# Gated linear attention heads: when a weight chunk is rounded, when each exponential signals, and the order of the gated output's chunks

## The reference, cut to what matters

```
q, k, v, r = split(h @ w_in)                      # 4 heads, dk = 128, dv = 256
log_a = log_sigmoid((h @ w_a1) @ w_a2 + b_a) / 16
b = cumsum(log_a)
scores[i,j] = sum_d q[i,d] k[j,d] exp(b[i,d] - b[j,d])    (j <= i)
o = scores @ v + (q * exp(b)) @ S ;  S_new = exp(b_last) * S + (k * exp(b_last - b))^T v
out = (rmsnorm(o, out_norm) * silu(r)) @ w_out ;  x = x + out
```

## Time and profile before

| | us |
|---|---|
| median of the timed runs | 2563.43 |
| lowest and highest of the three | 2563.18, 2563.78 |
| the profiled execution's own time | 2564.44 |
| its span, first to last instruction | 2562.7 |
| TensorE busy (share of the span) | 2506.0 (98%) |
| VectorE, ScalarE, GpSimd busy | 1640.9, 1054.4, 803.7 |

### The profile page before, as it was taken

One profiled execution on the slowest core, in us unless ns is written; L12 is line 12 of the kernel. 1 busy time (PEld: TensorE's weight loads), 2 busy tenths in 40 slices (PEclk: granted clock), 3 DMA queues, 4 the chain that ended last, 5 costly groups with the idle time before them and its releaser, 6 DMA issues.

```text
span 2562.7 us, 44016 instructions
## 1 busy us (share of the span) xinstructions
PE 2506.0 (98%) x18342; PEld 2426.2 (95%) x18342; DVE 1640.9 (64%) x2666; ACT 1054.4 (41%) x1737; POOL 803.7 (31%) x532
## 2 busy tenths in 40 slices
PE   8999999999999999999999999999999999999999
PEld 6899999998999999999998998999999999999999
DVE  6735353588676756774725786665697676748754
ACT  6433342473233333332537666445553233333322
POOL 5221222253444444003522214333434444441002
PEclk9999999999999999999999999999999999999999
DMA  3111111032332326352213444122223332336522
GB/s 113 40 34 40 34 40 50 24 111 82 109 108 95 124 94 217 111 168 76 72 36 111 138 177 164 60 85 76 74 69 98 112 109 97 122 113 224 168 80 82
DMA packets 229682, 252.25 MB, mean 98 GB/s; under 512 B 16849, under 2 KB 178271, under 8 KB 228591
## 3 DMA queue, kind: packets, MB, share of 16 engines
q1 hardware_dynamic: 227087, 247.36, 29.4%
q10 hardware_dynamic: 2400, 2.10, 0.3%
HBM read 173.54 MB, written 75.89 MB: 97 GB/s over the span
## 4 chain that ended last, share of the span: by engine, by line
PE 79%; DVE 14%; issue 3%; ACT 2%; DMA 1%; SPq 0%; POOL 0%; DVEq 0%; ACTq 0%; POOLq 0%
PE ps L905 13%; PE ps L907 13%; PE ps L906 13%; PE ps L348 8%; PE ps L350 8%; PE ps L349 8%; PE ps L2836 3%; PE ps L2821 1%; PE ps L1713 1%; PE ps L1714 1%; PE ps L1715 1%; DVE xT L1432 1%; PE ps L1726 1%; DVE hflat L493 1%; PE ps L1808 1%
## 5 line engine op out<-in xcount | busy, mean ns | idle before, releaser
L1580 POOL TENSOR_TENSOR wlo<-wraw,whi 128x1024 fp32r<-128x1024 f32 x78 | 192.4, 2466 | 440.1 <-DVE s_raw L1267 440.1
L905 PE MATMUL ps<-hh,whi 128*128 128x264 f32 x928 | 264.8, 285 | 6.1 <-DVE wlo L1308 3.8
L313 POOL TENSOR_TENSOR wlo<-wraw,whi 128x2048 fp32r<-128x2048 f32 (+1 forms) x21 | 94.3, 4491 | 553.4 <-ACT whi L306 524.0
L906 PE MATMUL ps<-hl,whi 128*128 128x264 f32 x928 | 263.9, 284 | 0.0
L907 PE MATMUL ps<-hh,wlo 128*128 128x264 f32 x928 | 263.9, 284 | 0.0
L348 PE MATMUL ps<-hh,whi 128*128 128x352 f32 x648 | 218.8, 338 | 0.6 <-ACT cqr L3171 0.3
L592 DVE TENSOR_TENSOR xT<-xT,ps 128x352 f32<-128x352 f32 x288 | 147.2, 518 | 98.2 <-PE ps L350 97.7
L350 PE MATMUL ps<-hh,wlo 128*128 128x352 f32 x648 | 208.1, 321 | 0.0
L349 PE MATMUL ps<-hl,whi 128*128 128x352 f32 x648 | 207.9, 321 | 0.0
L905 PEld LDWEIGHTS ps<-hh,whi 128*128 128x128 f32 x928 | 174.7, 188 | 7.9 <-DVE wlo L1308 5.2
L1580 POOL TENSOR_TENSOR s_lo<-s_raw,s_hi 128x512 fp32r<-128x512 f32 x80 | 157.8, 1973 | 60.0 <-ACT s_hi L1101 60.0
(11 more groups left out here) (471 smaller groups left out, 8636.2 us busy)
## 6 DMA issues: line engine op xcount, KB each, us to landing
wraw<-w_ffn_in SPq DMA_DIRECT2D x88, 512.0 KB, 3.8
s_a<-hf SPq DMA_DIRECT2D x44, 528.0 KB, 3.2
wraw<-w_ffn_out SPq DMA_DIRECT2D x44, 512.0 KB, 3.8
s_t<-h SPq DMA_DIRECT2D x16, 1056.0 KB, 4.5
hflat<-s_t SPq DMA_DIRECT2D x16, 1056.0 KB, 6.0
h<-s_a SPq DMA_DIRECT2D x12, 1056.0 KB, 5.8
wraw<-w_gla_in SPq DMA_DIRECT2D x24, 512.0 KB, 4.5
s_x<-xT SPq DMA_DIRECT2D x6, 1408.0 KB, 5.5
```

What stands on the lines that cost most here:

```text
L313: pool.tensor_tensor(lo[:, 0:cols], raw[:, 0:cols], hi[:, 0:cols].bitcast(F32), ALU.subtract).then_inc(S("w_lo"), 1)
L905: nc.tensor.matmul(out, w_[0], x_[0], start=first, stop=False, skip_group_check=True)
L906: nc.tensor.matmul(out, w_[0], x_[1], start=False, stop=False, skip_group_check=True)
L1580: return pool.tensor_tensor(lo[:, cols], raw[:, cols], hi[:, cols].bitcast(F32), ALU.subtract)
```

## The change

On ScalarE each of the two exponentials of a level signals `lvl_exp`, so that the semaphore counts 14 a head; the split of `gc(h, 2)` stands between the exponentials of level 2 and `v_copy(3)`; and `ga_hi(1)` stands ahead of `silu(1, 2)`. On VectorE `lvl_qk` waits for the first exponential ahead of the queries' product and for the second ahead of the keys'; and the gated output is worked on in the order product 0, product 1, low 0, low 1, product 2, low 2. No instruction that computes is added or taken out.

```diff
@@ act_gla_decays
-            act.activation(v[:, :, hl_:2 * hl_], v[:, :, hl_:2 * hl_], ACT.Exp, scale=1.0 / TAU)
+            act.activation(v[:, :, hl_:2 * hl_], v[:, :, hl_:2 * hl_], ACT.Exp, scale=1.0 / TAU)\
+               .then_inc(S("lvl_exp"), 1)
             act.activation(v[:, :, 0:hl_], v[:, :, 0:hl_], ACT.Exp, scale=-1.0 / TAU)\
                .then_inc(S("lvl_exp"), 1)
@@ act_gla_head
                 act_gla_decays(act, h, n_)
-                v_copy(n_ + 1)
                 if n_ == 2:
                     act_split(act, gc(h, 2), WC)
+                v_copy(n_ + 1)
...
             ga_hi(0)
+            ga_hi(1)
             silu(1, 2)
-            ga_hi(1)
             ga_hi(2)
@@ lvl_qk
-                dve.wait_ge(S("lvl_exp"), h * 7 + n_ + 1)
+                dve.wait_ge(S("lvl_exp"), h * 14 + 2 * n_ + 1)
...
                 dve.tensor_tensor(scaled[:, :, hl_:2 * hl_], blocks(gq[:, 0, :], hl_, n)[:, :, hl_:2 * hl_],
                                   e[:, :, hl_:2 * hl_], ALU.mult)
+                dve.wait_ge(S("lvl_exp"), h * 14 + 2 * n_ + 2)
@@ dve_gla_head
-            for j in range(NCH):
+            def gated(j):
...
+            def gated_low(j):
...
+            gated(0)
+            gated(1)
+            gated_low(0)
+            gated_low(1)
+            gated(2)
+            gated_low(2)
```

## The result

The changed kernel takes 2549.29 us (median of 5 runs, 2548.74 to 2549.97) against 2563.58 for the kernel before (5 runs, 2563.18 to 2564.14): a ratio of 0.9943, 95% interval 0.9933 to 0.9954, 14.3 us less. I had forecast 2551.8, and 2549.5 to 2557.0 for the range: the direction and the places were right, the gain was 2.7 us larger than the sum of 11.6, and the median lies 0.2 us outside the range. Two single executions among the experiments, 4077 us in e6 and 6300 us in e11, are far outside all the others and count in no ratio. Its profiled execution took 2549.7 us with a span of 2547.9, where the one before had 2564.44 and 2562.7.

The account below looks back on a forecast made before the run. TensorE, busy 98% of the span, was taken as the bound, so only its waits could be gained: 8.3 + 0.6 + 2.7 = 11.6 us off the 2563.43 us median gives 2551.8 us; range 2549.5 to 2557.0.

Parts of the forecast that it names:

- The wait at level 3: Head 1: TensorE's 1.47 us wait, traced to ScalarE's split delaying the exponentials; moving the split removes it, 0.9 us to spare.
- Part 2: Levels: each exponential signals alone, queries' product starts some 0.54 us earlier; VectorE's extra wait priced at 0, at most 0.12.
- Heads 1 to 3: Waits at levels 3 and 4 hold 8.6 us; less 0.1 us left in each head, gain 8.3 us.
- Head 0: Levels with a scan behind every iteration: VectorE is the bound from level 3 on; gain 0.6 us, ends -0.5 and 3.3.
- Part 3: Gated output reordered: xT waits in the output projection go, 2.4 us plus 0.3 on top of four waits, 2.7 us.
- Given back: Rival: gains are waited out later, behind the heads; half left, 2557.6 us, or up to no change, 2563; chance 0.11.
- slower: Rival: GpSimd's eight subtractions each take their longest against VectorE's level products; 5.3 us slower, 2568.7 us; chance 0.03.
- not what it says: Rival: level 3's differences are late, not the split, so its exponentials start no earlier; held excluded, no chance given.
- The turns eat part 1: Rival, levels 3 and 4: VectorE's two-SBUF-input product also passes a subtraction, each level 0.65 us later; 2556.8 us, chance 0.20.

Follow-up runs that it names:

- e6: Kernel before with only VectorE's new order of the gated output, ScalarE's order as before: 2563.47 us.
- e11: Changed kernel with GpSimd's eight subtractions held back until level 5's products are made: 2547.38 us.
- e1: Kernel before with only the split of the r chunk moved ahead of v_copy(3): 2557.29 us.
- e2: Kernel before with only the signals changed, each exponential signalling alone: 2559.48 us.
- e0: Kernel before, unchanged, run again for a second profile: 2563.53 us.
- e13: Changed kernel, unchanged, run again for a second profile: 2549.71 us.
- e7: Changed kernel with GpSimd's low part of the r chunk in 4 subtractions of 512 columns instead of 8 of 256: 2550.48 us.
- e12: Changed kernel with five of head 0's six scans put behind the product with exp(b), eight subtractions kept: 2545.76 us.
- e9: Changed kernel with four of head 0's six scans, those behind iterations 2 to 5, moved behind the product with exp(b): 2548.57 us.
- e8: Changed kernel with the low part of the r chunk in 16 subtractions of 128 columns: 2547.79 us.

## Why the prediction was right, and where it was short

- **The wait at level 3, and its source**: right. The split fills the idle time in front of `v_copy(3)`, which starts on its tile; the exponentials start behind the copy; e1 without e2 leaves 0.18 us of the 1.47.
- **Part 2, the extra wait at no cost**: right. Between L2067 and L2072 no gap opened (0.78 + 208.66 = 209.44 against a start at 209.36). e2 alone gains 4.1 us.
- **Heads 1 to 3**: 8.3 forecast, 8.77 measured (3.02, 2.74, 3.01), 0.5 short. I had kept 0.1 us of wait at level 4 of each; nothing is left. Head 2's lower figure comes from a level 4 wait of only 0.52 us in the first profile of before; in the second (e0) it was 1.1, like the others, and the stage 0.3 longer.
- **Head 0**: 0.6 forecast, 1.24 and 1.15 measured, 0.6 short. "VectorE is the bound from level 3 on" was right only together with the turns: levels 4 to 6 of the changed kernel start 4.26 and 4.25 us apart, VectorE's pace, but in e11 levels 3 to 5 keep TensorE's 4.11 with every scan in place. This was the term with the widest ends, -0.5 to 3.3. Its upper end alone gives 2549.1 us, which is below my range (2549.5) and far below the 2550 of the forecast's own.
- **Part 3**: 2.7 us forecast, 3.4 measured between the first profiles (0.62, 0.63, 0.62, 1.49) and 3.6 alone. **This is the step that failed.** I wrote "0.3 for what comes on top of four waits", having worked out 0.25 us for each wait in the levels and used it for the six waits of heads 1 to 3 just before. Four waits make 1.0: the term is 3.4, as measured. The mechanism was right, and this term of the sum too small by 0.7 us.
- **The remainder**: 13.56 us of the 14.3 between the medians are gained up to the first L905 in the first two profiles, 0.19 of it ahead of head 0's levels, where the second profile of before stands 0.16 us the other way, so that is spread too. The other 0.7 is in no stage that the change touches. The second pair of medians (e13) does not have it: its gain is 13.4.
- **The sum**: 0.7 for part 3, 0.6 for head 0, 0.5 for heads 1 to 3, 0.2 and 0.7 of the remainder make the 2.7 us by which 11.6 fell short. With 1.0 in place of 0.3 the forecast would have been 2551.1. Whether the median came to lie just outside or just inside the range was luck, as the two sets of runs show; that part 3 came out at 2.7 was not.
- **Given back, slower, not what it says**: none. No new wait of TensorE has come in the heads. Behind them one has grown, at L348 for the low part of the latent queries, from 0.7 us to 0.4 and 1.6. It is the execution's and not the change's: nine of the 17 profiles have the one wait (0.6 to 0.7 us; e13 is among them), and just in these nine TensorE's granted clock falls to 1.2 GHz behind the wait of some 2 us ahead of it, so that its matmuls take up the time. From that wait to the last one it is 6.5 us in all 17. **The turns eat part 1**: no; L2075 with its two SBUF inputs never had to let a subtraction pass. The row of L2075 in the kernel after, min/median/max:

```profile
L2075 DVE TENSOR_TENSOR gqd<-gq,ge x16: 672/684/689, 73.9 to 464.1; 128x512 f32<-128x512 f32 x16
L2075 DVE TENSOR_TENSOR gkd<-gq,ge x12: 674/684/689, 78.2 to 460.6; 128x512 f32<-128x512 f32 x12
```

In e7 and e12 too its longest is 0.69 us. It follows L2072, which has just let one pass, and in head 1 it starts at 209.99 and GpSimd's next subtraction at 210.00, which then takes 1.27 us. The Trainium skill (SBUF — State Buffer, "SBUF: two separate sides") has it that whoever starts first, of a VectorE operation with two SBUF inputs and a GpSimd operation that reads SBUF, holds the shared pair of ports for the whole instruction. The 1.26 us of L2072 beside a 512-column subtraction and 0.42 beside a 128-column one agree with that.

The gaps between the rows say what a wait costs. In the output projection of head 1 before, TensorE's timeline around the wait is:

```profile
276.87 0.32 PE L349 MATMUL ps<-galo,whi 128*128 128x352 f32 x1
277.03 0.32 PE L350 MATMUL ps<-gahi,wlo 128*128 128x352 f32 x1
277.72 0.43 PE L348 MATMUL ps<-gahi,whi 128*128 128x352 f32 x1 [0.37 <-DVE xT L592]
277.99 0.33 PE L349 MATMUL ps<-galo,whi 128*128 128x352 f32 x1
```

Starts are 0.16 us apart without a wait, and 0.69 across it: 0.53 later, of which the idle column has 0.37, as it begins at the end of a matmul that overlaps the next by 0.16. The next start then comes 0.27 and not 0.16 behind. That is 0.64 us for an idle time of 0.37, and the stage gained 0.62. At the wait of 1.32 us in head 3 it is 1.5, 0.2 on top.

## What to carry to other kernels

Where matmuls overlap, price a wait of TensorE at the shift of the starts around it, not at the idle time beside it: here a wait was worth 0.2 to 0.3 us more, and once that is known it belongs on every wait in the sum. Where two engines take turns by whole instructions, follow the turns row by row in the order of both queues; my count of one turn for each operation gave too much in e7, and in e9 I had left out the scan that met one. And where one round of a loop carries extra work on the engine that is nearly the bound, look for its idle stretch first: moving five of head 0's scans (e12) was worth 2.5 us in that head by the profiles and 4 between the medians, beside the 14 of the change itself.

## What the runs showed of the hardware

A VectorE operation of 16 columns took 0.17 us alone, and 0.42, 0.71 and 1.26 us beside GpSimd subtractions of 128, 256 and 512 columns. GpSimd's own subtraction took 0.45, 0.72 and 1.27 us at the least for these sizes (the last at L2418 of the changed kernel; the chunk's own in e7 took 1.44 and more, beside VectorE). 128 columns more cost 0.27 us and 256 more 0.55, so about 0.2 us of each does not grow with its columns, an estimate from these three. The chunk took 8.8 us in 8 pieces (head 1) and 15.8 us in 16 (head 0 of e8), and was still in time. Two profiled executions of one kernel differed by 1.6 to 1.9 us in the 1988 us behind the heads, and by 0.6 and 0.7 us at the end of head 3. In five of 17 profiles a granted clock of 1.2 GHz for a part of one 5 us stretch (0.79 of full speed over it in before) went with 0.5 to 1.4 us more in the stage around it.
